# Routing of a two-layer decoder kernel: row blocks, row factors, filler products, a split gather signal and early weight requests

## The chip, the cores and the metric

The kernel runs on one core of one Trainium2 chip. Its time is what one execution takes on the device, in microseconds (us). The number that counts is the median over runs. A profile of one execution goes with it, and every row shown below is read from that profile, with times counted from the start of its span.

## What is computed

The reference is a decoder of two layers for a prompt of 256 rows and 8 samples of 4 rows, so 288 rows of 1024 columns. Each layer has a mixer (attention in three forms, and a recurrent branch) and a channel mixer. The channel mixer of layer 0 is a dense feed-forward block, that of layer 1 chooses two of eight experts for each row. Only the second matters here:

```python
def rmsnorm(x, g):            # rows scaled by 1/sqrt(mean square), then by the weights g
    ...
def moe_swiglu(h, router, w1, w3, w2):
    logits = (x @ router).astype(jnp.float32)
    top_val, top_idx = lax.top_k(logits, TOP_K)
    gate = jax.nn.softmax(top_val, axis=-1).reshape(-1)
    ...                       # rows are sorted by expert and padded to blocks of 128
    yd = lax.map(lambda a: swiglu(a[0], w1[a[1]], w3[a[1]], w2[a[1]]), (xd.reshape(n_blocks, MOE_BLOCK, d), blk_e))
    contrib = yd.reshape(-1, d)[dest] * gate[order][:, None]
    return jax.ops.segment_sum(contrib, tok[order], num_segments=n)
```

## The kernel before

All five engines have a program of their own, written out by hand in order, and they meet at semaphores. SyncE (SP) asks for the weights, GpSimd (POOL) for cache pages, the scatter of rows and the results. The order of the work on an engine is the order of the text.

The mixer of layer 1 ends in the product with w_out, eight blocks of 128 output columns (the loop over d in the tensor program). After each block VectorE (DVE) adds it to the residual xT (line 2219). by_tokens(k) turns block k of xT around, so that rows lie on partitions, and adds its part of the router's product. In the kernel before, by_tokens(d - 2) follows block d, and two calls are left behind the loop. ScalarE (ACT) squares and keeps the turned rows in two halves of 512 columns (square_rows, keep_rows into x2), and rounds weights in between.

Then the routing of layer 1 begins. The logits are copied (line 2288), turned (line 1282) and copied again; DVE ranks the experts of each row and writes the choice sel (signal sel_d). TensorE computes each row's place in its expert's block and the counts (signal pos_pe). DVE makes the normed rows h2 with rows_normed (line 2321: rows times the row's factor rsd times the norm's weights wffn), and with first_chosen (line 2327) the selection Sel0 for the first item, which is always expert 0 (signal x0_d). TensorE gathers the first item's 128 rows as a product of h2 and Sel0, 24 products of 128 columns, each issued as two instructions since the operands are fp32 (signal x_pe). ACT rounds the gathered block into Xh (item_high) and DVE takes the rest Xl (item_low, signal x_l). Meanwhile DVE computes where each row goes. POOL scatters h2 into token_slots by it (line 2673), and the list of items is written (signal items).

An item is 128 rows through one expert. The expert's weights come in units of 128x3072 or 128x2048 fp32 into a ring of six buffers. ACT rounds each unit (line 1403) into one of three high buffers, DVE takes the low part (line 1804), and TensorE multiplies high by high, high by low and low by high, 512 columns each. Units A are for the two up products, units C for the down product. The first item begins with four A units ahead of a loop (up(0, j, j)). The loop runs the other 20 units of an item and the first four of the next (BODY), and the last item stands behind it (LAST). There were seven passes and a last item here. used counts units that TensorE has finished. SP asks for unit u of the ring when used reaches u + 7. Units 0 to 5 of the ring are asked for while w_out runs; the next ones (numbered 0 on from LEAD, two of them already among the six) follow only after SP has read the list of items, since the loop's requests name the expert by a register. AHEAD tells how many of the numbered units are asked for in front of the loop.

## Time and profile before

| | |
|---|---|
| median of 3 runs | 1766.36 us (1765.54 to 1767.7) |
| the profiled execution's own time | 1767.29 us |
| its span | 1765.7 us (1.6 us lie around it) |
[...]
| TensorE busy | 1699.4 us, 96% |
| DVE, ACT, POOL busy | 62%, 48%, 10% |
| chain that ended last, by engine | PE 89%, DVE 6%, ACT 2%, DMA 2%, issue 1% |
| bytes moved | 424.95 MB, mean 241 GB/s |

The profile has a page (busy time, the span in 40 slices, the chain that ended last, the costliest groups) and views that answer questions: the chain in order of time, the timeline of an engine, busy time and granted clock in chosen stretches, and who waited for whom. [...]

### The profile page before, as it was taken

The page shows a single profiled execution, that of the slowest core. Times are in us where ns is not written, and L with a number is a line of the kernel's source. Part 1 is how long each engine was busy: PE and PEld are TensorE (multiplying, and loading weights), DVE is VectorE, ACT ScalarE, POOL GpSimd, SP SyncE. Part 2 cuts the span into 40 slices and gives each one's busy share as a digit, 9 for nine tenths or more (in the row PEclk, how much of TensorE's full clock was granted, in tenths as well). Part 3 has the DMA queues.
Part 4 walks back from the last instruction along what each step waited for, and adds up shares of the span by engine and source line. Part 5 has one row for each costly group of instructions (what it writes and reads, how often), then busy time and mean ns, then how long its engine had stood idle before and what let it go on. Part 6 is the DMA issues. An engine that isn't in the chain of part 4 may idle for free.

```text
span 1765.7 us, 23577 instructions
## 1 busy us (share of the span) xinstructions
PE 1699.4 (96%) x8772; PEld 1394.1 (79%) x8772; DVE 1099.3 (62%) x1289; ACT 841.9 (48%) x900; POOL 176.3 (10%) x237
## 2 busy tenths in 40 slices
PE   7999999999999999999998999999999999999997
PEld 4877677689999897767765788888888888888884
DVE  1563423546654355342345488888888888888887
ACT  2342332034343233332203467677777777777764
POOL 1421012200000242101220100000000000000030
PEclk9999999999999999999998899999999999999999
DMA  9649143355544684224255689999999999999993
GB/s 246 166 156 286 49 108 84 131 163 168 167 152 159 149 244 129 86 65 120 72 161 204 239 323 393 373 381 392 358 403 352 400 351 399 350 397 353 399 388 109
DMA packets 232202, 424.95 MB, mean 241 GB/s; under 512 B 34462, under 2 KB 129982, under 8 KB 231932
## 3 DMA queue, kind: packets, MB, share of 16 engines
q1 hardware_dynamic: 219292, 383.62, 62.4%
q0 software_dynamic: 12832, 40.28, 7.2%
q8 instruction: 49, 0.80, 0.2%
q14 instruction: 29, 0.24, 0.0%
HBM read 403.70 MB, written 24.29 MB: 242 GB/s over the span
## 4 chain that ended last, share of the span: by engine, by line
PE 89%; DVE 6%; ACT 2%; DMA 2%; issue 1%; DVEq 0%; SPq 0%; ACTq 0%
PE ps L753 85%; PE ps L757 4%; DVE weights_low L1804 2%; DVE arena L1804 2%; ACT weights_high L1403 2%; DMA weights_in<-in_moe_w 1%; DVE arena L2026 1%; DMA arena<-in_vecs 0%; DVEq L2417 0%; DVE arena L2525 0%; ACT arena L1403 0%; DVE arena L2321 0%; DVE arena L1953 0%; DVE arena L1934 0%; ACT arena L1400 0%
## 5 line engine op out<-in xcount | busy, mean ns | idle before, releaser
L1804 DVE TENSOR_TENSOR weights_low<-weights_in,weights_high 128x3072 fp32r<-128x3072 f32 (+1 forms) x192 | 589.3, 3090 | 105.5 <-ACT weights_high L1403 105.3
L753 PE MATMUL ps<-arena 128*128 128x288 f32 (+16 forms) x2732 | 578.8, 368 | 29.5 <-DMA arena<-in_vecs 8.9
L1403 ACT ACTIVATE weights_high<-weights_in 128x3072 fp32r<-128x3072 f32 (+1 forms) x192 | 489.6, 2560 | 197.1 <-PE ps L753 169.1
L753 PEld LDWEIGHTS ps<-arena 128*128 128x128 f32 (+7 forms) x2732 | 420.6, 180 | 168.6 <-issue 65.0
L753 PE MATMUL ps<-weights_high,item_high 128*128 128x512 f32 x704 | 278.2, 395 | 7.2 <-DVE weights_low L1804 6.6
L753 PE MATMUL ps<-weights_high,item_low 128*128 128x512 f32 x704 | 274.6, 390 | 0.0
L753 PE MATMUL ps<-weights_low,item_high 128*128 128x512 f32 x704 | 274.6, 390 | 0.0
L1400 ACT ACTIVATE arena<-arena 128x128 f32<-128x128 f32 (+12 forms) x191 | 75.5, 409 | 188.4 <-DVE arena L1804 84.3
L753 PEld LDWEIGHTS ps<-weights_high,item_high 128*128 128x128 f32 x704 | 132.6, 188 | 36.1 <-DVE weights_low L1804 8.9
L753 PEld LDWEIGHTS ps<-weights_high,item_low 128*128 128x128 f32 x704 | 132.6, 188 | 28.0
L753 PEld LDWEIGHTS ps<-weights_low,item_high 128*128 128x128 f32 x704 | 132.7, 189 | 26.5
L753 PE MATMUL ps<-weights_high,gated_high 128*128 128x512 f32 x352 | 138.8, 394 | 3.9 <-DVE gated_low L1804 3.4
L753 PE MATMUL ps<-weights_high,gated_low 128*128 128x512 f32 x352 | 137.7, 391 | 0.0
L753 PE MATMUL ps<-weights_low,gated_high 128*128 128x512 f32 x352 | 137.7, 391 | 0.0
L1403 ACT ACTIVATE arena<-ps 128x256 f32<-128x256 f32 (+10 forms) x138 | 59.8, 465 | 160.8 <-PE ps L757 124.3
L1804 DVE TENSOR_TENSOR arena<-ps,arena 128x256 f32<-128x256 f32 (+8 forms) x104 | 42.6, 426 | 131.4 <-PE ps L753 129.1
L757 PE MATMUL ps<-arena 128*128 128x128 f32 (+5 forms) x613 | 96.1, 287 | 16.7 <-DVE arena L1804 10.6
L757 PEld LDWEIGHTS ps<-arena 128*128 128x128 f32 (+5 forms) x613 | 73.5, 145 | 46.9 <-DVE arena L1804 20.8
L1400 ACT ACTIVATE arena<-ps 128x288 f32<-128x288 f32 (+3 forms) x78 | 44.1, 566 | 132.9 <-PE ps L753 119.0
L753 PE MATMUL ps<-rows_high,ffn_high 128*128 128x288 f32 x352 | 104.6, 297 | 0.0
L753 PE MATMUL ps<-rows_low,ffn_high 128*128 128x288 f32 x352 | 103.8, 295 | 0.0
L753 PE MATMUL ps<-rows_high,ffn_low 128*128 128x288 f32 x352 | 103.5, 294 | 0.0
(205 smaller groups left out, 1870.2 us busy)
## 6 DMA issues: line engine op xcount, KB each, us to landing
weights_in<-in_moe_w SPq DMA_DIRECT2D x192, 768.0 KB, 8.3
weights_in<-in_moe_w SPq DMA_DIRECT2D x48, 1536.0 KB, 9.7
weights_in<-in_moe_w SPq DMA_DIRECT2D x64, 512.0 KB, 4.9
ffn_in<-in_ffn_w SPq DMA_DIRECT2D x30, 1024.0 KB, 7.1
weights_in<-in_moe_w SPq DMA_DIRECT2D x16, 1024.0 KB, 9.6
arena<-in_w_in SPq DMA_DIRECT2D x32, 384.0 KB, 4.1
arena<-in_w_in SPq DMA_DIRECT2D x32, 256.0 KB, 4.9
token_slots<-arena SPq DMA_DIRECT2D x12, 512.0 KB, 7.5
```

Source lines behind the costliest of these rows:

```text
L753: return nc.tensor.matmul(out, lhsT, rhs, start=start, stop=stop)
L757: return nc.tensor.transpose(out, x, ident[0:k, 0:k])
L1400: return nc.scalar.activation(out, x, f, **kw)
L1403: return nc.scalar.activation(out, x, ACT.Copy, scale=scale)
L1804: return V.tensor_tensor(out, x, y, op)
L2026: V.tensor_reduce(nm[:, i % 2, :], x, AX.X, ALU.max, negate=True).then_inc(nm_ev.sem, 1)
```

## The change

It does eight things.

- by_tokens(d - 1) instead of by_tokens(d - 2) follows block d of w_out, from d = 1 on; one call instead of two is left behind the loop.
- rows_normed is gone. rows_weighted_ffn multiplies the rows by the norm's weights alone, in two halves of 512 columns and three row tiles: half 0 behind the last residual add of the w_out loop, half 1 behind the logits' last step. The row's factor goes into the selection of item 0 (selr = sel times rsd, one small operation), and into h2 by three products on POOL (128x1024 each) ahead of the scatter. POOL starts these when the gather is done (x_pe at 2).
- awake(n): n products of 128x128 with 128x288, into a bank that nobody reads, six behind the turned logits and three behind the counts.
- The gather signals x_pe after each half (four of eight blocks), ACT and DVE round it in halves of 512 columns, and TensorE waits for the first half ahead of unit 0 and for the second ahead of unit 2. Later items wait with counts that are one higher.
- AHEAD is 6 instead of 2: SP asks for numbered units 2 to 5 by fixed code with expert 0 (waiting for used 9 to 12) before it waits for items.
- The signals of the dense products' rounding are merged from four semaphores into two, with the same order and the same waits.
- keep_rows(0) signals xt1_ev.
- One more column group of working memory (selr).

```diff
-AHEAD = 2
+AHEAD = 6
@@ tensor, loop over d of w_out
                     if d >= 2 and l == 0:
                         norm(1, d - 2, d - 1)
-                    elif d >= 2:
-                        by_tokens(d - 2)
+                    elif d >= 1 and l == 1:
+                        by_tokens(d - 1)
...
-                    by_tokens(KD - 2)
+                    def awake(n):
+
+                        for i in range(n):
+                            mm(ps[:, 1, 0:N], ident, xT[:, i, :])
+
                     by_tokens(KD - 1)
...
                     i.then_inc(lg_pe.sem, 1)
+                    awake(6)
                     pe.wait_ge(xt2_ev.sem, xt2_ev.at(0))
                     pe.wait_ge(sel_d.sem, sel_d.at(0))
...
                     i.then_inc(pos_pe.sem, 1)
+                    awake(3)
                     pe.wait_ge(x0_d.sem, x0_d.at(0))
...
-                    i.then_inc(x_pe.sem, 1)
+                        if k % 4 == 3:
+                            i.then_inc(x_pe.sem, 1)
...
-                    pe.wait_ge(x_l.sem, 1)
                     for j in range(LEAD):
+                        if j % 2 == 0:
+                            pe.wait_ge(x_l.sem, 1 + j // 2)
@@ scalar
-                    item_high(0)
+                    for b in range(2):
+                        act.wait_ge(x_pe.sem, b + 1)
+                        copy(Xh[:, 4 * b:4 * b + 4, :].rearrange("p k s -> p (k s)"), ps[:, 4 + b, :]).then_inc(x_h.sem, 1)
@@ vector
+                def rows_weighted_ffn(i):
+
+                    done = (xt1_ev, xt2_ev)[i]
+                    dve.wait_ge(done.sem, done.at(0))
+                    for m in range(3):
+                        n, x = ROWS[m], slice(512 * i, 512 * i + 512)
+                        tt(h2[0:n, m, x], x2[0:n, m, x], wffn[0:n, x], ALU.mult)
...
+                    if l == 1 and d == 7:
+                        dve.wait_ge(wf_in.sem, wf_in.at(0))
+                        rows_weighted_ffn(0)
...
-                        return V.tensor_scalar(Sel0[0:n, m, :], c("iota")[0:n, :], dest[0:n, m, 0:1], sel[0:n, m, 0:1],
+                        return V.tensor_scalar(Sel0[0:n, m, :], c("iota")[0:n, :], dest[0:n, m, 0:1], selr[0:n, m:m + 1],
                                                ALU.is_equal, ALU.mult)
-                    dve.wait_ge(wf_in.sem, wf_in.at(0))
-                    dve.wait_ge(xt2_ev.sem, xt2_ev.at(0))
-                    rows_normed(0)
+                    tt(selr, sel[:, :, 0], rsd, ALU.mult)
+                    rows_weighted_ffn(1)
                     dve.wait_ge(pos_pe.sem, pos_pe.at(0))
...
-                    first_chosen(0).then_inc(x0_d.sem, 1)
-                    rows_normed(1)
-                    first_chosen(1).then_inc(x0_d.sem, 1)
-                    rows_normed(2)
-                    first_chosen(2).then_inc(x0_d.sem, 1)
+                    for m in range(3):
+                        first_chosen(m).then_inc(x0_d.sem, 1)
@@ sync
+                    for u in range(2, AHEAD):
+                        kind, ch, j = BODY[u]
+                        sp.wait_ge(used.sem, u + 7)
+                        unit(0, kind, ch, j, (LEAD + u) % NRAW)
                     sp.wait_ge(items.sem, items.at(0))
@@ gpsimd
             pool.wait_ge(x0_d.sem, x0_d.at(0))
+            pool.wait_ge(x_pe.sem, 2)
+            for m in range(3):
+                n = ROWS[m]
+                x = rsd[0:n, m:m + 1]
+                nc.gpsimd.tensor_tensor(h2[0:n, m, :], h2[0:n, m, :], bass.AP(x.tensor, x.offset, [x.ap[0], [0, D]]), ALU.mult)
+            pool.drain()
             pool.wait_ge(dst_d.sem, dst_d.at(0))
```

## Rows read from the trace of the kernel before

**Rows 1.** Chain that ended last, routing of layer 1: start, length, engine, line.
```profile
959.78 2.25 PE ps L753 x18
...
965.72 15.07 PE ps L753 x48
...
980.81 1.03 ACT item_high L1403
...
981.87 1.24 DVE item_low L1804
...
983.15 14.57 PE ps L753 x58
...
997.81 2.79 ACT weights_high L1403
...
1003.98 0.88 DVE arena L1804
...
1004.90 0.87 PE ps L757 x6
```

**Rows 2.** Stretches of the routing: busy (count) by engine, then clock, DMA share, GB/s.
```profile
955.70:959.00 3.30, 0.31 (x3) 0.22 (x3) 2.57 (x13) 3.28 (x10) 0.00 (x0) 1.00 1.04 422
959.20:965.70 6.50, 2.24 (x18) 2.07 (x18) 5.51 (x16) 0.89 (x2) 0.00 (x0) 0.51 0.03 11
965.72:980.79 15.07, 15.07 (x50) 11.47 (x50) 4.49 (x11) 0.00 (x0) 0.00 (x0) 0.50 0.00 1
983.20:986.30 3.10, 3.10 (x7) 2.42 (x8) 2.42 (x19) 0.00 (x0) 0.80 (x1) 0.50 0.03 5
```

**Rows 3.** Who waited, 980 us to the end: total, times, longest us.
```profile
PE ps L753 <- DVE weights_low L1804: 7.0, 10, 0.9
```

**Rows 4.** Timeline, DVE at the w_out loop and the logits' copy.
```profile
923.80 0.46 DVE L2219 SCALAR_TENSOR_TENSOR arena<-ps,arena 128x288 f32<-128x288 f32 x1 [3.42 <-PE ps L753]
...
947.63 0.46 DVE L2219 SCALAR_TENSOR_TENSOR arena<-ps,arena 128x288 f32<-128x288 f32 x1 [4.53 <-PE ps L753]
...
952.62 0.46 DVE L2219 SCALAR_TENSOR_TENSOR arena<-ps,arena 128x288 f32<-128x288 f32 x1 [0.35 <-PE ps L753]
...
955.65 0.46 DVE L2288 COPY arena<-ps 8x288 f32<-8x288 f32 x1 [2.26 <-PE ps L753]
```

**Rows 5.** DVE groups by shape, 840 to 1000 us: count, busy us, mean ns.
```profile
L1804 DVE TENSOR_TENSOR weights_low<-weights_in,weights_high 128x3072 fp32r<-128x3072 f32 x5 | 16.8, 3355 | 4.4 <-ACT weights_high L1403 4.4
...
L1804 DVE TENSOR_TENSOR arena<-arena 128x288 f32<-128x288 f32 x8 | 3.7, 459 | 0.6
```

**Rows 6.** Timeline of DVE, the normed rows' second product and the last selection.
```profile
962.69 1.28 DVE L2321 SCALAR_TENSOR_TENSOR arena<-arena 128x1024 f32<-128x1024 f32 x1
...
965.34 0.33 DVE L2327 TENSOR_SCALAR arena<-arena 32x128 f32<-32x128 f32 x1
```

**Rows 7.** Stretches elsewhere, columns as in rows 2.
```profile
279.80:283.20 3.40, 2.68 (x16) 1.94 (x15) 0.53 (x2) 0.41 (x1) 0.89 (x1) 1.00 0.05 11
283.40:286.50 3.10, 3.10 (x10) 2.25 (x10) 0.77 (x4) 0.20 (x1) 2.69 (x2) 0.51 1.00 242
831.20:832.60 1.40, 1.40 (x13) 1.40 (x14) 0.37 (x3) 0.72 (x4) 0.60 (x1) 1.00 0.97 298
```

**Rows 8.** Timeline, a POOL product and a DVE operation beside it.
```profile
877.38 1.92 POOL L2651 TENSOR_TENSOR arena<-arena 128x1032 f32<-128x1032 f32 x1 [3.11 <-PE ps L753]
...
878.25 1.06 DVE L2157 SCALAR_TENSOR_TENSOR arena<-arena 32x1 f32<-32x1 f32 x1
```

**Rows 9.** Timeline of SP's requests and of the items' list.
```profile
989.44 0.15 DVE L2406 CAST items<-ps 1x13 int32<-1x13 f32 x1
...
993.17 0.39 SPq L699 DMA_DIRECT2D weights_in<-in_moe_w  x1
...
1121.02 4.46 SPq L705 DMA_DIRECT2D weights_in<-in_moe_w  x2
...
1129.86 0.37 SPq L699 DMA_DIRECT2D weights_in<-in_moe_w  x1
```

More of the change, by code:

```diff
@@ L350, in dense_low, with rows_split, piece_split @@
             return dense_piece(i, mlow[(1, 2, 0, 1)[i // 2]][:, :])
+        def rows_split(k):
+            return k + 1 + k // 4
+        def piece_split(i):
+            return 5 if i == 0 else 9 + i
         def dense_high(i):
@@ L387, in build @@
         nbB = rtake(P)
-        gmx, gsum, fss, frs, rsd = (rtake(3) for _ in range(5))
+        gmx, gsum, fss, frs, rsd, selr = (rtake(3) for _ in range(6))
         fsq = rtake(6).rearrange("p (m i) -> p m i", m=3)
@@ L1417, in norm @@
                     act.wait_ge(h_ev.sem, h_ev.at(idx, k + 1))
-                    copy(mTh[k], hT[:, k, :]).then_inc(dh_ev.sem, 1)
+                    copy(mTh[k], hT[:, k, :]).then_inc(dense_h.sem, 1)
                     if k == 3:
@@ L1431, in dense_rounded @@
                     act.wait_ge(event.sem, event.at(l, n))
-                copy(dense_high(i), dense_raw(i)).then_inc(wh_ev.sem, 1)
+                copy(dense_high(i), dense_raw(i)).then_inc(dense_h.sem, 1)
             act.wait_ge(vt_pe0.sem, vt_pe0.at(0))
@@ L1753, in _ @@
                     square_rows(0)
-                    keep_rows(0)
+                    keep_rows(0).then_inc(xt1_ev.sem, 1)
                     high_first(1)
@@ L1831, in dense_rows_low @@
             def dense_rows_low(l, k):
-                dve.wait_ge(dh_ev.sem, dh_ev.at(l, k + 1))
-                tt(mTl[k], hT[:, k, :], mTh[k].bitcast(F32), ALU.subtract).then_inc(dl_ev.sem, 1)
+                dve.wait_ge(dense_h.sem, dense_h.at(l, rows_split(k)))
+                tt(mTl[k], hT[:, k, :], mTh[k].bitcast(F32), ALU.subtract).then_inc(dense_l.sem, 1)
             def dense_rest(l, i):
-                dve.wait_ge(wh_ev.sem, wh_ev.at(l, i + 1))
-                tt(dense_low(i), dense_raw(i), dense_high(i).bitcast(F32), ALU.subtract).then_inc(wlo_ev.sem, 1)
+                dve.wait_ge(dense_h.sem, dense_h.at(l, piece_split(i)))
+                tt(dense_low(i), dense_raw(i), dense_high(i).bitcast(F32), ALU.subtract).then_inc(dense_l.sem, 1)
             dve.wait_ge(w8_pe.sem, w8_pe.at(0))
@@ L2362, in item_low @@
                     def item_low(w):
-                        dve.wait_ge(x_h.sem, w + 1)
+                        dve.wait_ge(x_h.sem, w + 2)
                         tt(Xl.rearrange("p (b k) s -> p b (k s)", b=2), ps[:, 4:6, :],
                            Xh.rearrange("p (b k) s -> p b (k s)", b=2).bitcast(F32), ALU.subtract).then_inc(x_l.sem, 1)
-                    item_low(0)
+                    for b in range(2):
+                        dve.wait_ge(x_h.sem, b + 1)
+                        tt(Xl[:, 4 * b:4 * b + 4, :].rearrange("p k s -> p (k s)"), ps[:, 4 + b, :],
+                           Xh[:, 4 * b:4 * b + 4, :].rearrange("p k s -> p (k s)").bitcast(F32), ALU.subtract).then_inc(x_l.sem, 1)
                     dve.wait_ge(nb_pe.sem, nb_pe.at(0))
@@ L2679, in _ @@
             with pool.Fori(0, n1) as w:
-                pool.wait_ge(x_pe.sem, w + 1)
+                pool.wait_ge(x_pe.sem, w + 2)
                 pool.dma_start(xin, xi[w + 1]).then_inc(xin_in.sem, 16)
```

21 lines of the change are left out of this document (8 added, 13 removed).

## The prediction

> **What bounds the kernel now.** I read the page first, then the chain that ended last, then the stretches of the routing. TensorE is busy for 96% of the span, so time can only come from its few idle or slow stretches. The largest is the routing of layer 1 [rows 1]. The logits are there at 955.65 [rows 4], yet the expert products start at 983.15, and after the first four units TensorE stands again until 1004.90. The reader should see two things. TensorE has little to do while DVE ranks and makes the rows, 3.3 us with 0.31 busy and then 6.5 us with 2.24 busy [rows 2]. And the granted clock falls to 0.5 in it and stays there: the gather takes 15.07 us at 0.50 without a gap, and the clock is still at 0.50 in the first 3.1 us of unit 0 [rows 2]. Behind 1005 there is nearly nothing to win: TensorE waited 7.0 us in all for low parts, at most 0.9 at once [rows 3]. It works on in step with its own earlier end, so what the routing gains stays, as long as weights arrive.
>
> **The change part by part.** All is counted against the profiled execution (1767.29 us, 0.93 above the median 1766.36).
>
> *Rows one block behind.* Before, a block's DVE add follows the last one by 3.42 + 0.46 = 3.88 us where no by_tokens stands between, and by 4.53 + 0.46 = 4.99 where one does [rows 4]: a by_tokens costs TensorE 1.11 us. TensorE has no gap in this loop, so one call moved forward leaves the end of the last call, about 955.6, where it was: gain 0. The last add moves from 952.62 to 953.73 and ends at 954.19, ahead of the last by_tokens (it starts at 953.73 + 1.06). ACT gets the first half about 3.9 us earlier, which nobody waits for.
>
> *Factors folded in.* A 512-wide product on DVE isn't in the trace. From 459 ns for 288 columns and 3355 for 3072 [rows 5] the slope is 1.04 ns a column, so 0.69 us, three in a row about 1.95. Half 0 stands on DVE behind the last add and ahead of the logits' copy: 954.19 + 1.95 + 0.2 for the three fills = 956.3 against 955.65. Behind the waiting copy hangs all of the routing, so this costs 0.65 (0 to 1.1). Choice and counts then start at 960.4, not 959.78. Behind them, before, the second and third row product lay open up to the last selection at 965.34 [rows 6], with TensorE starting at 965.72 [rows 1]. Now: choice 0.4 for logits and factor, 0.1 for selr, 1.95 for half 1, 0.4 copies, 0.9 for three selections: the gather can start at 963.95. Net -1.75 (-1.0 to -2.2).
>
> *Fillers.* awake(6) is 12 instructions, awake(3) 6. A block of w_out is 16 of the same shape in 3.88 us, 0.243 each, so 2.9 and 1.45 us at full clock, twice that at half. The six start at 957.2 and end at 960.1, just ahead of the choice. The counts' 18 instructions took 2.25 us at about half clock [rows 1]; at full clock I take 1.15, to 961.55. The three end at 963.0, ahead of 963.95. So they hide completely at full clock. What they buy is the clock: no idle stretch above about 1.6 us is left where 3.3 and 6.5 us were nearly empty. The first idle (955.65 to 957.2, with tiny products in it) is the weakest spot; the next is 963.0 to 963.95.
>
> *Gather at full clock.* 48 instructions in 15.07 us at 0.50 are 0.314 each. Halved that is 7.5; a run of the same shape elsewhere at 1.00 has 13 in 1.40, 0.11 each [rows 7], or 5.2 for 48, but the gather changes between tiles of 128 and 32 rows. I take 7.0 (5.2 to 15.07): end at 970.95. Gain -8.1. The small products behind it were partly hidden and are now open, 0.95 us (half of the 1.75 they took at half clock; 0.9 to 1.75).
>
> [...]
>
> *Halves signalled.* Before, ACT's 1.03 and DVE's 1.24 with their gaps lay open between gather and unit 0, 980.79 to 983.15, 2.36 us [rows 1]. Now the first half is rounded during the second half's gather. DVE has the rest of unit 2 (3.36) in front of it, from about 965.5 to 968.9, and ends the half at 969.6, ahead of 971.9. The second half is ready at 972.3, and unit 2 needs it 8 us later. So unit 0 starts at 971.9, 11.25 us earlier. That is the sum of -1.75, -8.1 and 2.36 - 0.95 = 1.4 less.
>
> *From unit 0 to the first turn.* Before, 983.15 to 1004.90, 21.75 us [rows 1]. It is paced by ACT and DVE: unit 0, unit 1, unit 2 (about 4.1 each at full clock), then rounding 2.79, rest 3.36, product 0.88 [rows 1, 5]. That is 12.3 + 7.1 = 19.4, with starts 19.6. So 2.15 more goes if the clock is full from the start.
>
> *POOL's three products.* They start with the gather's end, 970.95, and take 1.92 each [rows 8], to 976.7. Scatter and the load of the second item's rows follow; they are needed only late in the first pass, behind 16 units. But DVE's small chain to the items' list (starting 972.3, 1.5 us long before) now lies beside them. The row: a DVE operation of 32x1 took 1.06 us, from 878.25 to 879.31, beside a POOL product that ran from 877.38 to 879.30 [rows 8]; it ended when POOL did. If each such operation is held, the chain ends between 976.7 and 977.6, while TensorE wants it at 976.0 behind unit 0. Cost 0.9 (0 to 1.6).
>
> [...]
>
> *Four more units asked for.* Before, SP asked first at 993.17, 3.7 us behind the items' list at 989.44 [rows 9]; ACT had to wait for no DMA there. Now the requests follow units 0 to 3 (976 to 989) and the list is read later. Gain 0, since ACT's and DVE's pace decides; what it does is give cover for the earlier scatter. In each pass SP's loop turn now falls ahead of an A unit behind two C units, 1121.02 to 1129.86 [rows 9], where there is more room. The merged semaphores keep order and waits: 0.
>
> **The sum.** Unit 0 at -11.25, to the turn -2.15, POOL +0.9: -12.5 us. 1767.29 - 12.5 = 1754.8, and from the median 1753.9. I say 1754.0. With bounds taken together (-10 to -14.5), 1752 to 1756.5.
>
> **The rivals.**
> - *The clock is held only in part.* It falls in one of the short waits or in the gather's middle; half of the gather at 0.50 costs 4. For it: narrow tiles of 32 rows in the gather, and the fall behind a stretch that was mostly busy [rows 7]. Time 1757 to 1762.
> - *The clock falls ahead of the gather.* Then it stays at 0.50 through it, as before. What is left is -1.75 and 0.6 of the small products: about -2.3, 1764. For it: the fall in rows 7; against: the wide fillers on both sides.
> - *The change doesn't do what it says: fillers in the way.* The clock falls before the six, and they run at 0.5: 5.8 us from 957.2 to 963.0, counts 2.25, then 2.9: gather at 968.2 against 965.72. Less 0.6, that is +1.9: 1768.3. Against it: the idle ahead is 1.6 us.
> - *Slower: SP's loop turn.* Place: ahead of the A unit behind two C units, seven times. Price: a turn of 3.7 us [rows 9] with no slack is 7 x 3.7 = 26 us, so 1780. It decides only from the point where a turn is longer than the 4.4 us from one request to the next plus the wait of a landed unit for its rounding. Against it: the turn lay between two requests and made neither late.
>
> **How the numbers follow.** Forecast 0.68; clock held in part 0.12; clock falls ahead of the gather 0.12; fillers in the way 0.05; slower 0.03. The range 1750.5 to 1762 takes the first two, the bounds and about 1 us of other stretches' clock falls, 0.8. A measurement can tell 0.2%, 3.5 us. Faster by more: 0.68 + 0.12 = 0.80. Within: 0.12 + 0.05 = 0.17. Slower: 0.03.
>
> **What would show it.** The clock at 1.00 from 955 to 1005; the gather in 6.8 to 7.6 us; the logits' copy 0.65 later against the last add; unit 0's start near 972 and the turn near 992.4; a gap behind unit 0 while POOL multiplies; then passes of the same length as before. It would be wrong if the gather shows 0.5, or if passes grow because units land late.

## The result, and the profile after

| | before | after |
|---|---|---|
| median of the executions, us | 1766.61 (17) | 1757.24 (17) |
| lowest to highest, us | 1763.14 to 1778.91 | 1752.07 to 1768.48 |
| profiled execution, us | 1767.29 | 1755.59 |
| its span, us, and mean granted clock | 1765.7, 0.982 | 1754.0, 0.991 |

The ratio of the times is 0.9943, with a 95% interval of 0.9923 to 0.9962: faster by 9.4 us in the median, where 12.4 was forecast (1754.0). The two profiled executions are 11.70 us apart, for a forecast of 12.5. That pair flatters the forecast: the one before lies 0.68 us above its median, the one after 1.65 us below. In the changed kernel mm is at L764, the transposes at L768 and L1297, ACT's copies at L1422, tensor_tensor at L1825.

Where the 11.7 us are is read against the first residual add of w_out, which stands at 919.92 us before and at 919.14 after (0.78 us of difference have come up to there). First DVE's timeline: the first and the last of these adds, and the logits' copy (columns as in rows 4).

```profile
919.14 0.46 DVE L2248 SCALAR_TENSOR_TENSOR arena<-ps,arena 128x288 f32<-128x288 f32 x1 [4.24 <-PE ps L764]
...
952.95 0.46 DVE L2248 SCALAR_TENSOR_TENSOR arena<-ps,arena 128x288 f32<-128x288 f32 x1 [1.26 <-PE ps L764]
...
955.57 0.46 DVE L2320 COPY arena<-ps 8x288 f32<-8x288 f32 x1
```

The copy is 36.43 us behind the first add; it was 35.73. The last add is 33.81 us behind the first, for 32.70 before, the 1.11 us of the forecast. Then TensorE's timeline through the routing: transposes of the logits, the six fillers, counts and three fillers (24 in one row), gather with the small products (58), the items' list, the first turn of the loop.

```profile
956.08 0.31 PE L1297 MATMUL ps<-arena 8*128 8x8 f32 x3 [1.20 <-DVE arena L2320]
956.32 3.18 PE L764 MATMUL ps<-arena 128*128 128x288 f32 x12
959.69 3.13 PE L764 MATMUL ps<-arena 128*128 128x8 f32 x24 [0.19 <-DVE arena L1825]
963.05 9.63 PE L764 MATMUL ps<-arena 128*128 128x128 f32 x58 [0.23 <-DVE arena L2353]
...
972.60 0.50 PE L764 MATMUL ps<-weights_high,item_high 128*128 128x512 f32 x1
...
977.80 0.23 PE L764 MATMUL ps<-arena 8*1 8x12 f32 x4 [0.82 <-DVE arena L1825]
...
993.63 0.88 PE L768 MATMUL ps<-arena 128*128 128x128 f32 x6 [3.11 <-DVE arena L1825]
```

Nothing ahead of the gather is longer than 1.20 us of idleness, where rows 1 and 2 had two nearly empty stretches. Unit 0 starts at 972.60, 10.55 us earlier than before, of which 9.77 came up behind the first add (53.46 us behind it for 63.23); the turn is 74.49 us behind the first add, where it was 84.98. The same in stretches, with the granted clock, as a share of full speed, in the column behind the five engines (columns as in rows 2):

```profile
955.60:959.60 4.00, 3.42 (x15) 2.42 (x15) 3.12 (x17) 3.38 (x7) 0.00 (x0) 1.00 1.03 416
959.60:963.00 3.40, 3.13 (x24) 2.38 (x24) 3.25 (x15) 0.40 (x2) 0.00 (x0) 1.00 0.04 14
963.05:971.58 8.53, 8.53 (x50) 6.60 (x50) 5.09 (x12) 0.60 (x1) 0.00 (x0) 1.00 0.01 3
...
990.60:993.60 3.00, 0.00 (x0) 0.00 (x0) 2.98 (x2) 2.99 (x3) 2.95 (x1) 1.00 1.02 401
994.40:997.80 3.40, 3.40 (x11) 2.68 (x10) 3.40 (x2) 0.81 (x1) 3.10 (x2) 0.53 1.03 414
```

The clock is 1.00 from 955.6 us to the turn. It falls only behind the 3.11 us in which TensorE stands ahead of the turn, to 0.53 for 3.4 us (it is 1.00 up to 994.55 and 0.50 from 994.6 on, so that stretch holds a little of both); those cost about half of 3.4, 1.7 us (an estimate). From the turn to the end of the span it is 760.4 us after and 760.8 before, and the longest waits for low parts are still at most 0.9 us (the waits from 980 us to the end, as in rows 3):

```profile
PE ps L764 <- DVE weights_low L1825: 6.8, 10, 0.9
```

That the end doesn't show the 1.7 us has to do with a second place. TensorE waits once for a low part of another kind (gated_low), 3.40 us before and 3.42 after, near the end of the last item. Behind it the clock fell in the execution before and not in the one after, which gives the 1.7 us back:

```profile
1744.40:1747.80 3.40, 3.40 (x10) 2.63 (x9) 1.43 (x2) 0.00 (x0) 0.00 (x0) 0.50 0.00 0
...
1733.90:1737.30 3.40, 3.40 (x17) 2.78 (x16) 1.87 (x2) 0.00 (x0) 0.00 (x0) 1.00 0.00 0
```

So 0.78 + 10.49 + 0.4 = 11.7 us: nearly all of it lies in the routing.

### The profile page after: what moved, and what is told of

The parts are those of the page before. It is cut to its first block, busy times and chain, and to the rows that moved or that the text cites. A ratio compares the mean times of both kernels' runs of the same rounds, so it can differ in the third digit from the quotient of the medians.

```text
span 1754.0 us, 23592 instructions
## 1 busy us (share of the span) xinstructions
PE 1692.9 (97%) x8790; PEld 1389.5 (79%) x8790; DVE 1102.4 (63%) x1294; ACT 842.1 (48%) x901; POOL 193.5 (11%) x240
## 4 chain that ended last, share of the span: by engine, by line
PE 86%; DVE 6%; DMA 4%; ACT 2%; issue 1%; DVEq 1%; SPq 0%; ACTq 0%
PE ps L764 82%; PE ps L768 4%; DMA weights_in<-in_moe_w 3%; DVE arena L1825 2%; DVE weights_low L1825 2%; ACT weights_high L1422 2%; DVE arena L2047 1%; DMA arena<-in_vecs 0%; DVEq L2442 0%; DVE arena L2550 0%; ACT arena L1422 0%; ACT arena L1419 0%; DVE arena L1974 0%; SPq L706 0%; DVE arena L2406 0%
## 5 line engine op out<-in xcount | busy, mean ns | idle before, releaser
L1825 DVE TENSOR_TENSOR weights_low<-weights_in,weights_high 128x3072 fp32r<-128x3072 f32 (+1 forms) x192 | 589.3, 3089 | 104.1 <-ACT weights_high L1422 103.0
L764 PE MATMUL ps<-arena 128*128 128x288 f32 (+15 forms) x2750 | 573.1, 364 | 24.1 <-DMA arena<-in_vecs 8.9
L1422 ACT ACTIVATE weights_high<-weights_in 128x3072 fp32r<-128x3072 f32 (+1 forms) x192 | 489.6, 2560 | 197.1 <-PE ps L764 171.0
L764 PEld LDWEIGHTS ps<-arena 128*128 128x128 f32 (+6 forms) x2750 | 415.7, 176 | 162.5 <-issue 58.6
L764 PE MATMUL ps<-weights_high,item_high 128*128 128x512 f32 x704 | 278.2, 395 | 6.4 <-DVE weights_low L1825 6.4
L764 PE MATMUL ps<-weights_high,item_low 128*128 128x512 f32 x704 | 275.2, 391 | 0.0
L764 PE MATMUL ps<-weights_low,item_high 128*128 128x512 f32 x704 | 274.8, 390 | 0.0
L764 PEld LDWEIGHTS ps<-weights_high,item_high 128*128 128x128 f32 x704 | 132.7, 188 | 35.1 <-DVE weights_low L1825 8.7
L764 PEld LDWEIGHTS ps<-weights_high,item_low 128*128 128x128 f32 x704 | 132.6, 188 | 28.0
L764 PEld LDWEIGHTS ps<-weights_low,item_high 128*128 128x128 f32 x704 | 132.6, 188 | 26.5
L764 PE MATMUL ps<-weights_high,gated_high 128*128 128x512 f32 x352 | 138.2, 393 | 3.8 <-DVE gated_low L1825 3.4
L764 PE MATMUL ps<-weights_high,gated_low 128*128 128x512 f32 x352 | 137.3, 390 | 0.0
L764 PE MATMUL ps<-weights_low,gated_high 128*128 128x512 f32 x352 | 137.1, 390 | 0.0
L1422 ACT ACTIVATE arena<-ps 128x256 f32<-128x256 f32 (+10 forms) x138 | 59.8, 465 | 160.3 <-PE ps L768 125.3
L1825 DVE TENSOR_TENSOR arena<-ps,arena 128x256 f32<-128x256 f32 (+8 forms) x104 | 42.6, 426 | 127.1 <-PE ps L764 124.7
L768 PE MATMUL ps<-arena 128*128 128x128 f32 (+5 forms) x613 | 97.3, 290 | 17.0 <-DVE arena L1825 10.9
L768 PEld LDWEIGHTS ps<-arena 128*128 128x128 f32 (+5 forms) x613 | 74.7, 146 | 47.0 <-DVE arena L1825 21.5
L764 PE MATMUL ps<-rows_high,ffn_high 128*128 128x288 f32 x352 | 104.7, 298 | 0.0
L764 PE MATMUL ps<-rows_low,ffn_high 128*128 128x288 f32 x352 | 104.0, 295 | 0.0
L764 PE MATMUL ps<-rows_high,ffn_low 128*128 128x288 f32 x352 | 103.6, 294 | 0.0
```

The lines of the kernel that those rows point to most:

```text
L764: return nc.tensor.matmul(out, lhsT, rhs, start=start, stop=stop)
L768: return nc.tensor.transpose(out, x, ident[0:k, 0:k])
L1422: return nc.scalar.activation(out, x, ACT.Copy, scale=scale)
L1825: return V.tensor_tensor(out, x, y, op)
```

## The experiments

All changes are to the changed kernel unless it is said otherwise. The kernel before was timed beside each group on the same chip; its medians were 1768.09 (first group of four), 1768.89 (second) and 1771.83 us (third). The changed kernel itself wasn't timed again in them. So a few us between medians of different groups, or between their ratios, say little; kernels of one group and places in the traces are the surer comparison. In the first group are the kernels without fillers, before with fillers, with GpSimd's products later and with all waits filled; in the second those with the requests as before, one signal, the factors on DVE, and there and back; in the third the other four.

### What the fillers do

**All fillers out.**

```diff
-                    awake(6)
...
-                    awake(3)
```

> The changed kernel without its nine filler products. Theory (the fillers hold the clock, and the clock is most of the gain): the granted clock falls to 0.5 ahead of the gather in every run, the gather takes 15.1 us, unit 0 starts 7 us later and runs at 0.5 for its first 3 us, and the median is 7 to 8 us above the changed kernel's 1757.2, so about 1764.5, only 2 us below the kernel before. Rival (the shorter chain, the split signal and the earlier requests bring the gain, and the clock would hold by itself now that the waits are shorter): the gather takes 8.5 us as in the changed kernel and the median stays within 1.5 us of 1757.2.

Measured: 1769.11 us (12 executions), ratio 1.0005 (0.998 to 1.003). All of the gain is gone from the median, 4.6 us more than the theory expected. The stretches of its trace:

```profile
956.06:959.60 3.54, 0.31 (x3) 0.21 (x3) 2.72 (x16) 2.92 (x6) 0.00 (x0) 0.63 1.04 420
959.68:963.20 3.52, 2.23 (x18) 2.04 (x18) 3.25 (x14) 0.31 (x2) 0.00 (x0) 0.50 0.02 7
963.23:978.00 14.77, 14.77 (x48) 11.39 (x48) 5.17 (x12) 0.60 (x1) 0.00 (x0) 0.50 0.00 1
```

The gather starts at 963.23, within 0.2 us of where it started with fillers, and then takes 15 us. Unit 0 comes 7.4 us later against the first add, as expected. The missing us stand behind it: the clock falls at the turn again, and for longer.

```profile
1001.40:1008.20 6.80, 6.11 (x18) 5.04 (x19) 4.87 (x3) 1.97 (x2) 0.62 (x1) 0.50 1.03 418
```

The other seven edits do shorten the routing: the turn is 82.97 us behind the first add, 2.01 less than in the kernel before. But from the turn to the end it is 764.26 us, 3.5 more than before, where the clock didn't fall at the turn. Without fillers nothing of the change is left that the medians can tell. The fillers, which compute nothing, carry it.

The other profiled executions say the same of the gather. In five of the fourteen TensorE stands 1.3 us or more just ahead of it, and in all five the clock falls, ahead of it or 1.1 to 1.2 us into it. In the nine where it stands 0.23 us the gather runs at 1.00.

**The kernel before with nothing but the fillers.**

```diff
+                    awake(6)
                     pe.wait_ge(xt2_ev.sem, xt2_ev.at(0))
...
+                    awake(3)
                     pe.wait_ge(x0_d.sem, x0_d.at(0))
```

(The definition of awake goes in too.)

> The kernel before with the nine filler products alone. Theory: six products end at about 959.3 us of the trace, the choice is there at 959.7, so they delay nothing; the three end at 962.4 and leave 3.3 us idle ahead of the gather at 965.7, more than the 0.2 us of the changed kernel. If the clock holds over that, the gather takes 8.5 us and the median is 8 us below the kernel before, 1758.5; if it falls there, part of the runs lose it, and the median lies between 1759 and 1766. Rival (fillers bring nothing by themselves, or lie in the way): 1766 or above, with the counts starting later than 959.8 us.

Measured: 1763.61 us (1758.54 to 1772.34, 12 executions), ratio 0.9975 (0.9958 to 0.9992). Six executions lie at 1758.5 to 1762.1, six at 1765.1 to 1772.3. The profiled one is of the second kind: with the row products still on DVE, TensorE stands 2.05 us ahead of the gather, and the clock falls 1.2 us into it (the row holds the first 30 of its 48 products).

```profile
969.60 8.53 PE L753 MATMUL ps<-arena 128*128 128x128 f32 x30 [2.05 <-DVE arena L2334]
```

In the medians fillers alone give 4.5 us, the other edits alone nothing, both 9.4. They aren't a sum: the folded factors shorten the wait that three fillers have to cover. More fillers in the old kernel's longer wait weren't tried.

**The last three fillers out.**

```diff
                     i.then_inc(pos_pe.sem, 1)
-                    awake(3)
                     pe.wait_ge(x0_d.sem, x0_d.at(0))
```

> The changed kernel without the three filler products between the counts and the gather; the six behind the logits' transposes stay. TensorE then stands for about 1.9 us ahead of the gather (0.23 us in the changed kernel). My theory: this wait alone is enough for the clock to fall in most executions, in the gather or right ahead of it, so that the 48 products of the gather take 13 to 15 us where they took 8.53: median 1763 us, a few executions near 1757. Rival, only the long wait of 3.3 us that the first six fill matters: 1757.2 us, the same as the changed kernel, with the gather at 8.5 us.

Measured: 1765.14 us (1756.64 to 1776.35, 12 executions), ratio 0.9974 (0.9943 to 1.0005). Two executions are at 1756.7, ten at 1762 and more. The first theory holds. The interval of the ratio reaches 1, but the two nearest kernels of its group, with the last three fillers in, are at 1753.34 and 1755.04 us. Ahead of the gather TensorE stands 1.88 us, and in the profiled execution the clock falls there:

```profile
963.71 14.84 PE L764 MATMUL ps<-arena 128*128 128x128 f32 x47 [1.88 <-DVE arena L2352]
```

```profile
960.35:963.70 3.35, 1.48 (x18) 1.29 (x18) 3.20 (x14) 0.31 (x2) 0.00 (x0) 0.84 0.02 7
963.71:978.78 15.07, 15.07 (x50) 11.48 (x50) 5.18 (x12) 0.60 (x1) 0.00 (x0) 0.50 0.01 2
```

The gather takes 15.07 us, to the hundredth what rows 1 show. It isn't enough to fill the long wait. The clock falls once more at the turn, for 3.4 us.

**The factors back on DVE.**

```diff
+                    rows_normed(0)
...
+                    first_chosen(0).then_inc(x0_d.sem, 1)
+                    rows_normed(1)
+                    first_chosen(1).then_inc(x0_d.sem, 1)
+                    rows_normed(2)
+                    first_chosen(2).then_inc(x0_d.sem, 1)
...
-                nc.gpsimd.tensor_tensor(h2[0:n, m, :], h2[0:n, m, :], ...)
```

> The changed kernel with the old way of the factors: VectorE's three row products (each 128 x 1024) stand between the selections again, and GpSimd's three products are gone. My theory: the gather starts about 1.9 us later against the first w_out addition (near 45.8 instead of 43.9 us), VectorE isn't held behind GpSimd any more, which gives back 0.8 us, so 1 to 2 us longer if the clock holds: 1758.5 us. The wait before the gather is longer by the same 1.9 us with the same filler products in it, so the clock may fall there in some executions, and then the time is 1764 us or more. Rival, GpSimd's products cost more than the row products did (VectorE held, scatter late): under 1756 us.

Measured: 1765.26 us (1756.84 to 1768.46, 12 executions), ratio 0.9974 (0.9953 to 0.9996). The gather starts 45.09 us behind the first add instead of 43.91, 1.2 us and not 1.9 later: without half 0 behind the last add the logits' copy is back at 35.77 us, 0.66 earlier, which the expectation had left out. TensorE stands 2.06 us ahead of it:

```profile
965.04 15.99 PE L764 MATMUL ps<-arena 128*128 128x128 f32 x58 [2.06 <-DVE arena L2356]
```

```profile
963.00:965.00 2.00, 0.00 (x0) 0.00 (x0) 2.00 (x6) 0.00 (x0) 0.00 (x0) 1.00 0.00 0
965.04:980.00 14.96, 14.96 (x54) 11.55 (x54) 5.26 (x13) 1.19 (x2) 0.00 (x0) 0.54 0.01 2
```

The direct price of the edit in this trace is 1.2 us less the 0.8 that VectorE isn't held any more, 0.4 us; the fall of the clock 1.1 us into the gather costs 5.7 in the gather alone (14.22 us for its 48 products, 8.51 in the changed kernel). The other kernels of its group with the factors folded in and the order of the gather unchanged are at 1756.2 and 1756.6 us. So the folded factors earn their gain mostly by making the wait short enough for three fillers.

### The halves, the requests, the rows

**One signal for the gather.**

```diff
-                        if k % 4 == 3:
-                            i.then_inc(x_pe.sem, 1)
+                    i.then_inc(x_pe.sem, 2)
```

> The changed kernel with the gather signalled once, at its end, instead of after each half (the counter goes up by 2 there). My theory: the halves let ScalarE's first copy and VectorE's first difference run beside the second half of the gather, so without them about half of each (0.60 and 0.69 us) and the second issue come back before unit 0: between 1.0 and 2.2 us longer, 1758.5 us. The wait before unit 0 grows by as much. Rival, VectorE is held behind GpSimd anyway, so that part of it is hidden: under 0.5 us. Rival, the clock falls in the longer wait before unit 0: 6 us or more, the granted clock 0.50 in the first unit's products.

Measured: 1756.23 us (1752.25 to 1768.15, 12 executions), ratio 0.9942 (0.9917 to 0.9967). No loss can be measured; my theory expected 1.0 to 2.2 us. The rival with the clock is seen too, in part: the profiled execution is one of the long ones (1767.95). The trace has unit 0 9.92 us behind the gather's start, against 9.55 in the changed kernel:

```profile
981.73 1.09 ACT L1421 ACTIVATE item_high<-ps 128x512 fp32r<-128x512 f32 x2 [11.35 <-PE ps L764]
...
983.10 0.50 PE L764 MATMUL ps<-weights_high,item_high 128*128 128x512 f32 x1 [0.30 <-DVE item_low L1824]
```

Unit 0 waits for the first half only, so 0.61 for ACT's half and 0.70 for DVE's are all that lies between, of which 1.0 is hidden behind the small products anyway. What gains is that the rounding is cut in two; that the gather signals in the middle is worth 0.37 us. (In this execution the clock fell in unit 0, to 0.51 from 984.4 to 987.7; its longest fall, at 0.50 from 254 to 271 us, stands some 700 us earlier, see below. The 1.3 us between gather and unit 0 hold only the small products.)

**Requests as before.**

```diff
-AHEAD = 6
+AHEAD = 2
```

> The changed kernel with AHEAD put back from 6 to 2, all else kept. My theory: the requests of four more weight units by fixed code cost and save nothing that counts, since the first of these requests only leave earlier (977.01 us of the changed kernel's trace, 993.17 before) and the loop's own are not on the chain: 1757 us, within 3 us of the changed kernel. Rival, the fixed code is worth its own time (loop turns of SP that came late for the first weights): 1760 us or more. Rival on the other side, the early requests disturb the queue ahead of the units: under 1754 us.

Measured: 1756.58 us (1751.84 to 1768.79, 12 executions), ratio 0.9941 (0.992 to 0.9961): no difference. SP's first request of this part stands at

```profile
981.65 0.39 SPq L706 DMA_DIRECT2D weights_in<-in_moe_w  x1
```

here, which is 64.0 us behind the first add, and at 977.01 or 57.9 us in the changed kernel. 6 us more or less make no unit late.

**The rows two blocks behind again.**

```diff
-                    elif d >= 1 and l == 1:
-                        by_tokens(d - 1)
+                    elif d >= 2:
+                        by_tokens(d - 2)
...
+                    by_tokens(KD - 2)
                     by_tokens(KD - 1)
```

> The changed kernel with the rows of layer 1 two blocks behind again, as before the change. My theory: TensorE has no gap in this loop, so the end of the last rows is where it was; the last w_out addition comes 1.1 us earlier, and with it VectorE's three 512-wide products, which no longer push the logits' copy back, so the copy is 35.7 to 36.4 us behind the first addition (36.43 in the changed kernel) and the time between 0.7 us less and the same: 1756.9 us. Rival, ScalarE gets the first half of the rows later, so that the three 512-wide products of VectorE start later and push the copy: 1758 us or more, the copy over 36.8 us behind the first addition.

Measured: 1753.34 us (1751.84 to 1758.0, 6 executions), ratio 0.9898 (0.9864 to 0.9932). The size is in the trace. The first add is at 916.18, and

```profile
951.91 0.46 DVE L2321 COPY arena<-ps 8x288 f32<-8x288 f32 x1 [0.48 <-PE ps L764]
...
959.40 9.83 PE L764 MATMUL ps<-arena 128*128 128x128 f32 x58 [0.23 <-DVE arena L2354]
```

so the copy is 35.73 us behind it, as in the kernel before, and the gather 43.22 instead of 43.91. Moving the rows one block forward costs 0.7 us, because it lets the last add, and DVE's three products behind it, end later. In this execution the 0.7 us doesn't reach the turn (74.44 us behind the first add for 74.49), since the clock falls to 0.50 ahead of unit 0, from 968.6 to 972.0. Apart from such falls, this part of the change is a small loss.

### GpSimd's products

**The three products behind the items' list.**

```diff
             pool.wait_ge(x_pe.sem, 2)
+            pool.wait_ge(items.sem, items.at(0))
             for m in range(3):
```

> The changed kernel with POOL's three row products behind the items' list instead of behind the gather, so that they no longer lie beside DVE's short operations. Theory (DVE stood still beside POOL, 973.3 to 977.5 us, and TensorE waited 0.8 us behind unit 0 for it): the chain of short operations takes 1.5 us instead of 4.8, the 0.8 us wait behind unit 0 is gone, and the turn comes 0.8 to 0.9 us earlier against unit 0's start. The median is 0.9 us lower, less than single runs scatter, so the trace has to show it. Rival (DVE's operations are long for another reason): their lengths, 1.82 and 1.74 us, stay, and so does the wait. A second effect to look for: POOL's products then lie beside DVE's 128x3072 low parts, which may become longer by up to 1.9 us each; then the turn comes later than before.

Measured: 1757.05 us (1753.92 to 1763.75, 6 executions), ratio 0.9949 (0.993 to 0.9968): the same. In the changed kernel DVE's chain to the items' list lies beside GpSimd's products, and two operations of it are held:

```profile
971.74 5.64 POOL L2698 TENSOR_TENSOR arena<-arena 128x1024 f32<-128x1024 f32 x3 [56.51 <-PE ps L764]
...
973.70 1.90 DVE L1825 TENSOR_TENSOR arena<-arena 128x48 f32<-128x48 f32 x1
975.67 1.74 DVE L2406 TENSOR_SCALAR arena<-arena 8x12 f32<-8x12 f32 x1
```

They take 0.19 and 0.22 us where GpSimd does nothing (in the trace of this run). The wait of 0.82 us behind unit 0 is theirs. Put behind the list, the products meet DVE's 128x3072 low parts, which decide the pace:

```profile
974.57 8.71 POOL L2699 TENSOR_TENSOR arena<-arena 128x1024 f32<-128x1024 f32 x3 [62.34 <-DVE items L2431]
```

```profile
976.88 12.88 DVE weights_low L1825 x3
```

The 0.82 us are gone, but three low parts take 12.88 us together, 2.8 us more: the first two, beside GpSimd's products, 4.65 and 5.04 us, the third, behind them, its usual 3.34. VectorE is held beside GpSimd as before, at a worse place, and the two cancel: the turn is 74.55 us behind the first add, for 74.49.

### The waits that are left

**The short wait and the turn filled too.** To the edit before come:

```diff
+                    awake(2)
                     pe.wait_ge(lgt_d.sem, lgt_d.at(0))
...
+                    for i in range(5):
+                        mm(ps[:, 5, 0:N], ident, xT[:, i, :])
                     pe.wait_ge(items.sem, items.at(0))
```

> e3 with two more places filled: two products ahead of the turned logits (1.2 us idle there) and five behind the first four units (3.1 us idle ahead of the first turn). Theory (what scatters the changed kernel's runs from 1752 to 1768 is the clock falling in one of the short waits that are left): the runs come closer together, the high ones at 1762 and above become fewer, the mean clock is 0.992 or 0.993 in most runs, and the median is 1752 to 1755. Rival (the scatter comes from elsewhere, as the kernel before has it too, 1763 to 1779): the runs scatter as far as the changed kernel's and the median is 1756 to 1757.

Measured: 1754.36 us (1752.67 to 1755.43, 5 executions), ratio 0.9925 (0.991 to 0.994). The median is 2.7 us under the same kernel without these products, which ran in the same group, but the two intervals overlap, and the two profiled executions are the other way round (1755.43 and 1754.42). What the trace shows is the place. Ahead of the turn TensorE is now busy for 2.14 of 3.7 us, and the clock doesn't fall behind it:

```profile
988.00:991.70 3.70, 2.14 (x9) 1.33 (x7) 3.70 (x3) 3.27 (x2) 3.40 (x2) 1.00 0.97 292
992.00:996.00 4.00, 4.00 (x22) 3.38 (x21) 3.87 (x2) 0.82 (x1) 3.81 (x1) 1.00 0.97 373
```

Over all fourteen profiled executions: with this wait of 3.1 us or more left as it was, the clock falls at it in nine of eleven, for 3.4 or 6.8 us; the two others are the kernel before and the one with the rows two behind. In the three with products in it (this one and two below) it doesn't fall.

**The gather there and back, GpSimd in halves.** With both waits filled, and GpSimd's products back ahead of the items' list:

```diff
+                        order = (0, 1, 2) if k % 2 == 0 else (2, 1, 0)
-                        for m in range(3):
+                        for m in order:
...
+            for v in range(2):
+                pool.wait_ge(x_pe.sem, v + 1)
                 for m in range(3):
...
+                    y = h2[0:n, m, v * 512:v * 512 + 512]
```

> The changed kernel with four edits: the gather goes through the row tiles there and back (0,1,2 then 2,1,0), so that TensorE changes between the 128-row and the 32-row tiles half as often; GpSimd's products are made in two column halves, each behind its half of the gather; two products of 288 columns fill the wait for the logits' copy; five fill the wait before the loop's first turn. My theory: the there-and-back order takes off some 8 changes of 0.2 us, 1.6 us of the 8.5 us gather at full clock; the halves take away the 0.8 us wait behind unit 0 without lengthening the 128 x 3072 low parts (3.36 us each, where they were 4.29 with the products put later); the filled waits hold the clock at 1.0 in every execution, worth 1.5 us at the turn against the best executions and more against the median: 1751 us, nearly the same in every execution. Rival, the half products delay VectorE's two differences by more than they save: 1754 us or more. Rival, the changes between tiles cost nothing in the new order: gather still 8.5 us, 1752.5 us.

Measured: 1757.86 us (1748.66 to 1760.47, 8 executions), ratio 0.9925 (0.99 to 0.995). Three executions are at 1748.7 to 1751.0, as expected, five at 1757.7 to 1760.5, and the profiled one (1758.11) is of these. Its routing is as expected: gather and small products take 8.28 us instead of 9.63, nothing waits behind unit 0, and the clock is 1.00 from 900 to 1030 us. The time is lost 700 us earlier, in the chain at the sample values of layer 0:

```profile
247.59 1.02 ACT arena L1426 x3
248.60 0.04 issue
248.65 16.05 PE ps L764 x54
```

The clock is 0.50 from 249.6 us to 269.9. The same 54 products behind the same 1.10 us wait, in the profiled execution of the changed kernel:

```profile
252.29 0.17 ACT arena L1422
252.46 0.04 issue
252.51 8.77 PE ps L764 x54
```

7.3 us between two executions, in code that none of these edits touches. The profiled execution of the kernel with one signal had it too (15.25 us); the ten others in which this wait isn't filled did not.

**That wait filled, alone and with the rest.**

```diff
                 def sample_values(t, bank, gate, gate_bank):

+                    if t == 0:
+                        for k in range(2):
+                            mm(ps[:, bank, 0:N], ident, hT[:, k, :])
                     pe.wait_ge(spt_ev.sem, spt_ev.at(l, t + 1))
```

> The changed kernel with two products of 288 columns put, in each of the two layers, into the 1.1 us wait ahead of the 54 products of the sample values (252.51 and 814.07 us of the changed kernel's trace), some 700 us ahead of the routing of layer 1; their results are overwritten. My theory: the changed kernel's own executions lie 8 us apart because the granted clock falls behind this wait in a part of them (54 products in 16.05 us where they otherwise take 8.77, seen in the profiled executions of two other kernels with the same code there), not because of the routing. So with the wait filled the executions from 1762 us on vanish, or nearly: median 1755 us, all but one within 1752 to 1760. Rival, the clock falls there for another reason than the wait: the same mixture as the changed kernel, a third of the executions at 1762 us or more. Rival, the remaining falls are those of the routing: as the last, but the 54 products take 8.77 us in the slow ones.

> The four edits of the version with the gather there and back, GpSimd's halves and the two filled waits of the routing, and with them the filled wait ahead of the sample values in both layers. That version had three executions at 1748.7 to 1751.0 and five at 1757.7 to 1760.5 us; the profiled one of the latter had the 54 products at 0.50. My theory: both causes together are gone, so the median is 1750 us and all executions lie within 1748 to 1753. Rival, the clock's fall near 250 us has another cause: median 1757 us again, two groups 8 us apart.

Measured: alone 1755.04 us (1751.95 to 1758.22, 6 executions), ratio 0.9903 (0.9869 to 0.9936); with the rest 1752.24 us (1749.85, 1750.94, 1752.04, 1752.43, 1754.89, 1760.21), ratio 0.9895 (0.9859 to 0.9931). None of the six of the first is at 1762 or more, where the changed kernel has six of 17, and one of the six of the second is 8 us above their median. The second theory had expected all six within 1748 to 1753. That points to the wait as the cause but doesn't settle it: two kernels without this edit, that with all of the routing's waits filled (5 executions) and that with the rows two behind (6), had none at 1762 us or more either. What is shown is the place and the price, 7.3 us, not that the fillers prevent it.

The version with the early wait and the four edits has the lowest median of those run, though 1.1 us under the kernel with the rows two behind is less than six executions each can tell. Its stretches:

```profile
963.05:970.23 7.18, 7.18 (x50) 6.09 (x50) 5.09 (x12) 0.60 (x1) 3.29 (x3) 1.00 0.01 3
977.60:998.00 20.40, 19.73 (x90) 15.98 (x89) 15.22 (x6) 13.63 (x8) 12.68 (x7) 1.00 1.02 399
```

The gather takes 7.18 us instead of 8.53, and TensorE is idle for 0.67 us in the 20 us around the turn, which comes 72.24 us behind the first add (74.49 in the changed kernel). Its low parts keep their 3.36 to 3.42 us. The rows two behind would take another 0.7 us; an estimate, as the two weren't tried together.

## Why the prediction was right, and where its sizes were off

**The mechanism holds.** The argument was that the clock is the loss in the routing, that a busy gather doesn't bring it back by itself, and that the fillers hold it if they cover the waits. Without fillers nothing is left of the gain in the median, and with the last three out the gather takes 15.07 us without a gap, at 0.50, as before.

**Part of the agreement is luck.** The forecast for the median was 1754.0, and it is 1757.24, within the range but 3.2 us off; 1754.8 for 1755.59 holds for one execution that is below its median. Three of the signs named ahead weren't met: the gather wasn't done in 6.8 to 7.6 us, the turn came at 993.63 and not near 992.4, and the clock wasn't at 1.00 up to 1005.

**Logits' copy, +0.65.** Measured +0.70, and shown to be the price of the rows one block behind: undone, it is gone.

**Start of the gather, -1.75.** Measured -1.89 (43.91 us behind the first add against 45.80). The forecast took 0.69 us for a 512-wide product on DVE and 1.95 for three; they took 1.87:

```profile
953.32 1.87 DVE L1825 TENSOR_TENSOR arena<-arena 128x512 f32<-128x512 f32 x3
```

**The gather, 7.0 us.** Measured 8.53, the largest mis-sized term: 6.5 us gained for 8.1, 1.5 of the 2.0 us that are missing up to the turn. I had halved the time at 0.50, which gives 7.5, and taken off more because a run of one shape went at 0.11 us each. In the trace of after the starts are 0.11 us apart within a shape; each step from a 128-row tile to a 32-row one or back makes two of them 0.20 to 0.21 apart, so it costs 0.19 more, and this gather does it 15 times (2.9 us, where my 5.2 us for 48 starts had none). In the trace of before, at 0.50, the same starts are 0.21 apart, and 0.35 and 0.37 at a change, 0.30 more: the price of a change shrinks less than the clock grows. The there-and-back order has 8 changes and takes 7.18 us, and 1.35 / 7 = 0.19 us for each change agrees with the starts.

**Halves, unit 0 at 971.9.** Measured 972.60; against the first add it is 9.77 us earlier than before, for a forecast of 11.25. From the gather's end it is 1.02 us against a forecast of 0.95. The reason that I gave is only in part right: cutting the rounding in two does it, the early signal 0.37 us of it.

**Unit 0 to the turn, 19.6 + 0.9.** Measured 21.03. The wait for what GpSimd's products hold cost 0.82 for 0.9. The rest is the units: from unit 0's start to ScalarE's rounding behind unit 2 it is 13.94 us, or 13.1 without that 0.82, where I had three times 4.1. From there rounding, rest and product take 7.1 us, as forecast.

**The sum.** To the turn -10.5 for -12.5; of the missing 2.0 us the gather is 1.5 and the units 0.5. What lies ahead of the first add (-0.78, with the clock at 0.50 for 23.9 us there instead of 27.3) and behind the turn (-0.4, a fall of the clock more at the turn and one less near the end) hid that in the total, so that 1755.59 looks closer to 1754.8 than the steps were. Neither is an effect of the change that a run shows.

**What the forecast didn't see.** The wait ahead of the turn was 3.11 us before and after. In the profiled execution of the kernel before the clock stayed at 1.00 behind it; in that of the changed kernel it falls, about 1.7 us. Why the two differ stays open. The clock had been back at 1.00 for 18 us in the first, but in the kernel before with fillers it had been back for 17 us, and there it falls at the turn. I had taken the stretch from unit 0 to the turn at full clock and didn't ask what stands at its end. Nor did it name the one wait of 3.40 us near the end of the last item, where a fall of the clock costs as much. With products in it no trace shows the fall; what that is worth in the median isn't settled by five and six executions. And the median lies 1.65 us above the profiled execution, since the changed kernel's executions spread over 16 us with the clock (mean clock 0.993 at 1752.07 us, 0.984 at 1768.48). The term of about 1 us for falls elsewhere was far too small: one place alone is worth 7.3 us.

**The rivals.** "The clock is held only in part" came true in one half: the gather ran at 1.00, its 32-row tiles included, but the clock fell in a short wait, the one ahead of the turn, and the median lies at the lower edge of the 1757 to 1762 named for it. "The clock falls ahead of the gather" is what the kernels with 1.9 to 2.1 us of idleness show, with seven, nine and ten of twelve executions at 1762 and more and medians of 1763.6 to 1765.3: its price (1764) was right, and the folded factors are what keeps the changed kernel from it. "Fillers in the way" and the SP loop didn't appear.

## What to carry to other kernels

Where the engine that bounds a kernel waits a few microseconds and then does a gap-free stretch at half clock, fill each wait with products into a bank that nobody reads, the short ones next to the long one too (here of 288 columns; no other width was tried): without nine filler products nothing of the gain was left in the median (1769.11 us), and without three of them, with 1.88 us of idleness, the clock fell ahead of the gather. Compare the stretches' clocks before comparing two profiled executions: one fall elsewhere moved them by 7.3 us here. An edit that shortens the work of another engine may earn more by shortening such a wait than by its own time, so test both together and each alone (the factors on DVE again cost 0.4 us directly and 5.7 us in a gather whose clock fell behind 2.06 us of idleness). Order small products so that the tile's row count changes seldom (8.53 us with 15 changes, 7.18 with 8), and look at what VectorE does beside GpSimd's products: moved away from its short operations and beside its long ones, they cost the same (the turn 74.49 and 74.55 us behind the first add).

## What the runs showed of the hardware

**GpSimd's DMA issues end behind VectorE's low parts.** The scatter's issues take 0.86 to 1.08 us before. After, they fall beside VectorE's low parts, tensor_tensor operations on weights_in and weights_high:

```profile
981.19 4.12 POOL L2704 DMA_INDIRECT token_slots<-arena,slots  x1 [0.30 <-issue]
985.62 3.85 POOL L2704 DMA_INDIRECT token_slots<-arena,slots  x1 [0.30 <-issue]
989.77 3.78 POOL L2704 DMA_INDIRECT token_slots<-arena,slots  x1 [0.30 <-issue]
993.86 0.86 POOL L2704 DMA_INDIRECT token_slots<-arena,slots  x1 [0.30 <-issue]
```

```profile
981.10 3.36 DVE L1825 TENSOR_TENSOR weights_low<-weights_in,weights_high 128x3072 fp32r<-128x3072 f32 x1 [0.98 <-DVE items L2431]
985.28 3.36 DVE L1825 TENSOR_TENSOR weights_low<-weights_in,weights_high 128x3072 fp32r<-128x3072 f32 x1 [0.81 <-ACT weights_high L1422]
989.36 3.36 DVE L1825 TENSOR_TENSOR weights_low<-weights_in,weights_high 128x3072 fp32r<-128x3072 f32 x1 [0.72 <-ACT weights_high L1422]
```

The first ends at 985.31, VectorE at 984.46: 0.85 us later, the length of a free issue. The second and the third do the same (989.47 and 988.64, 993.55 and 992.72: 0.83 later each). With GpSimd's products put later, issues of 1.79 and 2.84 us end 0.97 and 0.86 us behind VectorE's end. So these five issues end as if each waited for VectorE's operation and then took its own time. The fourth row began 0.27 us ahead of the next low part (994.13) and took its 0.86. The traces don't tell which part of an issue is held. It cost nothing, since the second item's rows are wanted much later.

**Two small VectorE operations end with GpSimd's products.** The 128x48 tensor_tensor (1.90 us for 0.19) ended at 975.60, GpSimd's second product at 975.54. The 8x12 tensor_scalar (1.74 us for 0.22), which has one tensor input and a scalar per partition beside it, stood beside GpSimd's third product and ended at 977.41, that product at 977.38.
